# Hybrid decoder step on one core: the prompt mixer and the sample mixer in one block

## The chip, the cores and the metric

The kernel runs on one core of a Trainium2 chip, in one launch. A core has TensorE (PE; its weight loads are shown as PEld), VectorE (DVE), ScalarE (ACT), GpSimd (POOL) and SyncE (SP), each with its own instruction stream, and 16 DMA engines that serve all their transfers. The engines meet only through semaphores: an instruction waits until a semaphore has reached a value, and adds to one when it is done. The metric is device time in microseconds (us); lower is better. A time is the median of several runs.

## The reference

One layer of a decoder, applied to a prompt of 512 tokens and to a sample group of 8 x 4 = 32 tokens, which share all weights:

```python
def trunk_layer(x, c, ada_w, ..., state):
    mod = (jax.nn.silu(c) @ ada_w + ada_b)[:, None, :]
    sh1, sc1, gt1, sh2, sc2, gt2 = jnp.split(mod, 6, axis=-1)
    h = rmsnorm(x, g_mix) * (1 + sc1) + sh1
    mix, new_state = token_mixers(h, w_in, w_out, gate_b, mh_g, sinks, conv_w, state)
    x = x + gt1 * mix
    h = rmsnorm(x, g_ffn) * (1 + sc2) + sh2
    x = x + gt2 * peer_ffn(h, wq, subkeys, u_tab, v_tab)
    return x, new_state
```

`token_mixers` multiplies the normalised rows by `w_in` (1024 x 3336), runs three mixers on the result (an mLSTM with a matrix memory C, windowed attention with a key and value cache, a short convolution), and multiplies their outputs by `w_out`. For the prompt the states start at zero; for the sample they are inputs. `peer_ffn` chooses 128 of 16384 experts for each token (8 heads, 16 each, by the best sums of two lists of key scores), takes the dot product of the token with each chosen row of `peer_u`, and sums rows of `peer_v` with weights made of these dots. Everything is float32. The outputs are the rows of both groups and their new states.

## The kernel before

The kernel has three parts, one after the other, each a block with an instruction stream for each engine: `mix_prompt` (four tiles of 128 tokens), `mix_sample` (one tile of 32 rows), and `experts` (all tokens). A block ends when every engine has drained and all have met at a barrier (its rows carry the line of the `with` that opens the block, 934 and 1493); the next block begins there.

**A tile** is the same work in prompt and sample. Its rows are normalised (`dve_rms`), transposed in two batches T_H0 and T_H1 into hT (`transpose_rows`), and multiplied by seven column chunks of `w_in`, named GATES, QZ, KZ, VZ, SVCB, CCCH and OZ (`project`, line 618, and `transpose_weights`). The chunks alternate between the two banks ps_z[0] and ps_z[1], so a chunk waits until the one two before it has been copied out. GATES is copied out by VectorE in `dve_front` (line 785), CCCH there as well (line 826). The weights stream through three slots, in the order of `Stream`; a load waits until the matmuls on the chunk three before it are done. The last step is the out product (`out_product`, line 674) into both banks and the residual on VectorE (`dve_residual`, lines 874 to 878), which signals x1_ready; SP then stores the rows.

**Work for the experts done ahead.** While the mixers run, the kernel also does a part of the expert work of prompt tile 0: it routes the tokens (`keys`, `pairs`) and takes the 128 dots (`dots`, line 333). Each dot needs a gather of 128 rows of `peer_u`, 512 KB, issued by POOL (`gather`, line 341) into one of eight row buffers; a buffer is free when the dot on it is done. This work is put into named gaps of VectorE's stream. What a gap holds is set by the tables KEYS_IN, PAIRS_IN and DOTS_IN at line 274. Gap "Z" of the last prompt tile holds the keys and pairs of head 7 and 6 dots. Of the sample's gaps, "A" holds 7 dots, "B" 6, "C" 5, "D" 3, "E" 8, "F" 5, "G" 5, "K" 6, "L" 9, "N" 12, "O" 12, "Z" 11. VectorE runs them where the code has them, so what stands behind a gap waits for its gathers.

**The border.** VectorE's last work in the prompt block is gap "A", the residual of tile 3 and gap "Z" (lines 1294 to 1296). ScalarE and VectorE have by then normalised the sample's rows, and SP has loaded its first three weight chunks. SP's last work is to store the prompt's states and x1 and to wait for all of it (lines 1064 to 1067). The prompt's C is copied to the lower half of hT (`cT_out`) to be stored. The sample block begins with gap "A" on VectorE, the transposes on TensorE, the small loads, the rows and the weight chunks VZ, SVCB, CCCH and OZ on SP, and the gathers on POOL. Further on, SP loads the sample's key and value cache into `scratch`, which the routing work had used, and the sample's memory C (line 1515) into a weight slot, when the matmuls on OZ are done. TensorE transposes it at line 1695.

## Time and profile before

| | us |
|---|---|
| median of 3 runs | 2055.93 |
| lowest, highest run | 2049.76, 2057.97 |
| span of the profiled execution | 2046.0 |
| TensorE, weight loads busy | 1616.0, 764.0 |
| VectorE busy | 1207.7 |
| POOL busy | 1134.0 |
| ScalarE busy | 476.3 |

The page gives one execution from its first to its last instruction; it gives no other time of that execution than this span. Lines are those of the kernel before. In a row of a timeline the first number is the start in us from the span's start, the second how long it took; what stands in square brackets is how long the engine was idle just before it, and what ended that. The prompt mixer fills the span until 497, the sample mixer from 509 to 713, the experts the rest.

### The profile page before, as it was taken

To read this page: it belongs to the slowest core of one execution; us is meant where nothing else is said; L and a number is where in the kernel's file an instruction comes from. 1 tells how busy PE (TensorE), PEld (TensorE's weight loads), DVE (VectorE), ACT (ScalarE), POOL (GpSimd) and SP (SyncE) were. 2 spreads that over 40 slices of the span, in tenths; PEclk is the share of its full clock that TensorE was granted. 3 is DMA by queue.
4 is the path that set the end of the run, shared out by engine and by line. 5 is a ranking of instruction groups with operands and counts; after the bars stand their busy time and mean duration, and the time that the engine had idled before them with its cause. 6 is when DMAs were issued, how large, how long until landed. Compare 5 with 4: busy or idle time off the path is not lost.

```text
span 2046.0 us, 20838 instructions
## 1 busy us (share of the span) xinstructions
PE 1616.0 (79%) x5461; PEld 764.0 (37%) x5461; DVE 1207.7 (59%) x3129; ACT 476.3 (23%) x1217; POOL 1134.0 (55%) x1168
## 2 busy tenths in 40 slices
PE   6979989983767457768888888788878789599966
PEld 1524546451126113223433344333433344255422
DVE  2222355867766701116767766677667689679972
ACT  1221313130101021212223222222222223223321
POOL 3000021322873555777777667767777677577773
PEclk8989999996775679998999989899999899899988
DMA  8795676896995599999999999999999999799995
GB/s 319 254 364 207 215 263 218 305 337 135 355 385 179 198 401 404 392 416 394 400 420 420 400 368 418 419 373 420 420 401 391 388 403 419 308 412 417 414 372 226
DMA packets 237575, 713.43 MB, mean 349 GB/s; under 512 B 23102, under 2 KB 49056, under 8 KB 237457
## 3 DMA queue, kind: packets, MB, share of 16 engines
q0 software_dynamic: 156672, 570.49, 71.2%
q1 hardware_dynamic: 80488, 140.73, 19.4%
q10 hardware_dynamic: 312, 1.07, 0.2%
q8 instruction: 36, 0.59, 0.1%
q14 instruction: 67, 0.54, 0.1%
HBM read 704.42 MB, written 8.25 MB: 348 GB/s over the span
## 4 chain that ended last, share of the span: by engine, by line
PE 19%; DMA 14%; DVE 12%; issue 7%; POOL 7%; ACT 5%; DVEq 0%; POOLq 0%; ACTq 0%
PE ps_y L2316 13%; DVE u_rows L2095 6%; DMA v_rows<-in_peer_v_dram,expert_idx_ring 5%; DMA v_rows<-in_peer_v_dram,tile_idx 5%; PE ps_r L2290 4%; POOL u_rows L1890 3%; DMA u_rows<-in_peer_u_dram,expert_idx_ring 3%; POOL v_rows L1896 2%; POOL v_rows L1904 2%; ACT wt_diag L1987 2%; PE ps_y L2331 2%; DMA v_rows<-in_peer_v_dram,sample_idx 1%; DVE key_scores_w L2106 1%; ACT L2002 1%; ACT L2033 1%
## 5 line engine op out<-in xcount | busy, mean ns | idle before, releaser
L2316 PE MATMUL ps_y<-v_rows,wt_diag 128*128 128x512 f32 x1664 | 796.9, 621 | 146.6 <-DMA v_rows<-in_peer_v_dram,expert_idx_ring 65.2
L2316 PEld LDWEIGHTS ps_y<-v_rows,wt_diag 128*128 128x128 f32 x1664 | 311.4, 197 | 571.1 <-issue 547.5
L1890 POOL DMA_INDIRECT u_rows<-in_peer_u_dram,expert_idx_ring x384 | 368.2, 959 | 164.7 <-issue 90.3
L2095 DVE CUSTOM_DVE_ANT_0 u_rows<-u_rows,ps_y 128x1024 f32<-128x1024 f32 x360 | 420.4, 1218 | 64.1 <-DMA u_rows<-in_peer_u_dram,expert_idx_ring 58.1
L1896 POOL DMA_INDIRECT v_rows<-in_peer_v_dram,expert_idx_ring x384 | 366.7, 955 | 120.2 <-issue 99.3
L341 POOL DMA_INDIRECT low_rows<-in_peer_u_dram,tile_idx x128 | 174.7, 1364 | 214.7 <-DVE tile_dots L333 148.5
L607 PE MATMUL ps_z<-w_stream,hT 128*128 128x512 f32 (+5 forms) x560 | 249.0, 602 | 36.9 <-DMA w_stream<-in_w_in_dram 19.7
L2331 PE MATMUL ps_y<-v_rows,wt_diag 64*64 64x512 f32 x1024 | 135.1, 645 | 57.4 <-DMA v_rows<-in_peer_v_dram,tile_idx 50.8
L333 DVE CUSTOM_DVE_ANT_0 low_rows<-low_rows,tile_rows 128x1024 f32<-128x1024 f32 x128 | 152.9, 1232 | 44.1 <-DMA low_rows<-in_peer_u_dram,tile_idx 31.9
L607 PEld LDWEIGHTS ps_z<-w_stream,hT 128*128 128x128 f32 (+1 forms) x560 | 100.9, 185 | 163.9 <-issue 132.6
L1904 POOL DMA_INDIRECT v_rows<-in_peer_v_dram,tile_idx x128 | 122.1, 954 | 71.8 <-PE ps_y L2331 44.6
L2290 PE MATMUL ps_r<-wq,hT_next 128*128 128x256 f32 (+1 forms) x512 | 123.2, 396 | 17.9 <-ACT hT_next L1968 17.9
L1987 ACT ACTIVATE wt_diag<-ident,wts 128x128 f32<-128x128 f32 x416 | 127.2, 388 | 25.1 <-DVE wts L2101 25.1
L2105 DVE MAX8 top<-key_scores 128x8 f32<-128x128 f32 x64 | 18.2, 285 | 187.6 <-ACT key_scores L1978 187.4
L2290 PEld LDWEIGHTS ps_r<-wq,hT_next 128*128 128x128 f32 x512 | 101.9, 200 | 47.7 <-issue 22.6
L1983 ACT ACTIVATE act_val<-dots 128x8 f32<-128x8 f32 x52 | 10.9, 209 | 444.4 <-DVE dots L2095 444.3
L885 POOL TENSOR_TENSOR z_cc_ch<-z_cc_ch 128x256 f32<-128x256 f32 (+1 forms) x5 | 7.0, 1409 | 190.1 <-DVE z_cc_ch L826 190.0
L2331 PEld LDWEIGHTS ps_y<-v_rows,wt_diag 64*64 64x64 f32 x1024 | 39.6, 140 | 146.9 <-issue 114.8
L2095 DVE CUSTOM_DVE_ANT_0 u_rows<-u_rows,h_cur 128x1024 f32<-128x1024 f32 x24 | 28.7, 1227 | 89.0 <-DMA u_rows<-in_peer_u_dram,expert_idx_ring 88.9
L688 PE MATMUL ps_z<-w_out,qT_kT 128*128 128x512 f32 (+1 forms) x160 | 76.0, 636 | 4.7 <-DVE low_rows L1214 4.7
L894 POOL TENSOR_TENSOR z_o<-z_o,mlstm_g 128x512 f32<-128x512 f32 (+1 forms) x5 | 7.2, 1431 | 82.5 <-ACT z_o L755 82.5
L1996 ACT ACTIVATE wt_diag<-half_ident,tile_dots 128x64 f32<-128x64 f32 x128 | 32.2, 335 | 81.8 <-PE ps_y L2331 81.3
(434 smaller groups left out, 1628.3 us busy)
## 6 DMA issues: line engine op xcount, KB each, us to landing
w_stream<-in_w_in_dram SPq DMA_DIRECT2D x25, 2048.0 KB, 12.8
w_stream<-in_ada_w_dram SPq DMA_DIRECT2D x12, 2048.0 KB, 12.8
w_stream<-in_peer_wq_dram SPq DMA_DIRECT2D x8, 1024.0 KB, 8.5
wq<-in_peer_wq_dram SPq DMA_DIRECT2D x4, 2048.0 KB, 42.2
w_stream<-in_w_in_dram SPq DMA_DIRECT2D x5, 1568.0 KB, 8.5
w_stream<-in_w_in_dram SPq DMA_DIRECT2D x5, 1536.0 KB, 17.5
u_rows<-in_peer_u_dram,expert_idx_ring POOLq DMA_INDIRECT x384, 7.4
v_rows<-in_peer_v_dram,expert_idx_ring POOLq DMA_INDIRECT x384, 7.9
```

The costliest lines, as they stand in the source:

```text
L333: self.nc.vector.tensor_tensor_reduce(self.rows[:, k % NB, :], self.rows[:, k % NB, :], self.X.h0[:, :], 1.0, 0.0, ALU.mult, ALU.add, self ...
L341: self.nc.gpsimd.indirect_dma_start(self.rows[:, k % NB, :], None, U, bass.IndirectOffsetOnAxis(self.keep["idx0"][:, k:k + 1], 0)).then_in ...
L607: mm = self.nc.tensor.matmul(X.ps_z[i % 2][0:n, 0:b - a], X.hT[:, kc, 0:n], X.wr[:, slot, kc, 0:b - a], start=(kc == 0), stop=(kc == KC - 1))
L688: mm = nc.tensor.matmul(X.ps_z[c][0:n, :], X.mixT[:, kc, 0:n], X.w_out[:, kc, c * 512:(c + 1) * 512], start=(i == 0), stop=(i == KC - 1))
L1890: g.indirect_dma_start(u_rows[:, j, :], None, U, bass.IndirectOffsetOnAxis(where[:, j:j + 1], 0))\
L1896: g.indirect_dma_start(v_rows[:, j, :], None, V, bass.IndirectOffsetOnAxis(where[:, j:j + 1], 0))\
L1904: g.indirect_dma_start(v_rows[:, j, :], None, V, bass.IndirectOffsetOnAxis(idx0[:, k:k + 1], 0))\
L1987: a(diag[:, par, j, :], K["ident"][:, :], ACT.Copy, scale=wts[:, par, j:j + 1])\
L2095: v.tensor_tensor_reduce(u_rows[:, j, :], u_rows[:, j, :], row[:, :], 1.0, 0.0, ALU.mult, ALU.add, dots[:, par, j:j + 1]).then_inc(s["u_us ...
L2290: mm = nc.tensor.matmul(ps_r[:, 0, 0:256], hT[:, kc, :], wq[:, kc, bass.ds(h * 256, 256)], start=(kc == 0), stop=(kc == KC - 1))
L2316: mm = nc.tensor.matmul(ps_y[:, c * 512:(c + 1) * 512], diag[:, par, j, :], v_rows[:, j, c * 512:(c + 1) * 512], start=(first and j == 0), ...
L2331: mm = nc.tensor.matmul(ps_q[b * HP:(b + 1) * HP, half, c * 512:(c + 1) * 512], diag[rows, i % 2, j + b, 0:HP], v_rows[rows, j + b, c * 51 ...
```

## The change

The sample mixer is no longer a block of its own. `mix_sample` returns a function for each engine, and the prompt block calls it where that engine's prompt work ends. In place of the barrier there are waits for what both parts use: TensorE waits for tile 3's x1_ready and pool_done before the first chunk; SP waits for x1's store before it loads the sample's rows over the same buffer, for the small states before it stores C_p, and for the routing (a_routed) before it loads the caches; ScalarE and VectorE wait for the stores of the prompt's states before they copy SVCB and GATES. C_p is stored from `dm` (d_matrix) in place of hT. On VectorE the copy of the upper half of hT, and with it `dve_front`, now stands ahead of gap "Z" of tile 3 and of the sample's gap "A", which are called from inside it (`behind_rows`).

```diff
-        self.cT_out = self.hT[:, 0:4, :]
+        self.cT_out = self.dm[:, :, :]
...
+SMALL_STATES = 4 + MH
...
         self.z_landed(act, SVCB)
+        if self.kind == "sample":
+            act.wait_ge(self.prompt["state_out"], 16 * (1 + SMALL_STATES))
...
-    def dve_front(self, dve, chain, K):
+    def dve_front(self, dve, chain, K, behind_rows=None):
...
         v.tensor_copy(X.hT[:, 4:8, 0:n], X.ps_t[:, :, 0:n]).then_inc(s["t_free"], 1)
+        if behind_rows:
+            behind_rows(dve)
         self.gap(dve, "B")
         self.z_landed(dve, GATES)
+        if self.kind == "sample":
+            dve.wait_ge(self.prompt["state_out"], 16 * (1 + SMALL_STATES))
...
+            sp.wait_ge(done, 16 * SMALL_STATES)
             sp.wait_ge(s["t_free"], NT * TB + 1)
             sp.dma_start(O["C_p"].rearrange("l b h v k -> v (l b h) k"), X.cT_out).then_inc(done, 16)
             store(NT - 1)
             load_row(sp, nc, mod, X.row_g, 2, True, S.s["small_in"])
-            sp.wait_ge(done, 16 * (5 + MH))
-            sp.wait_ge(s["x1_stored"], 16 * (1 + NT))
+            sample["sync"](sp)
+            sp.wait_ge(done, 16 * (1 + SMALL_STATES))
...
             A.gathers(pool, U, NT - 1, "Z")
+            sample["gpsimd"](pool)
...
+            sample["scalar"](act)
...
                 T.dve_residual(dve, chain)
-                T.gap(dve, "Z")
+                if more:
+                    T.gap(dve, "Z")
...
+            def left_of_last_tile(eng):
+
+                T = tile(NT - 1)
+                T.chain0 = chain0
+                T.gap(eng, "Z")
+
+            sample["vector"](dve, left_of_last_tile)
...
+            pe.wait_ge(s["t_free"], NT * TB + 1)
+            sample["tensor"](pe)
...
-    with nc.Block() as block:
-        @block.sync
-        def _(sp):
+    def on_sync(sp):
...
+        sp.wait_ge(before["x1_stored"], 16 * (1 + NT))
+        sp.dma_start(X.xr[0:NS, :], I["x_sample"].rearrange("b t d -> (b t) d")).then_inc(s["xr_in"], 16)
+        for i in range(RING, len(CHUNKS)):
+            X.stream.load(sp, I, "sample", i)
+        sp.wait_ge(before["a_routed"], PH)
+        sp.dma_start(kc, I["cache_swa_k"][0].rearrange("b w h d -> w b (h d)")).then_inc(s["k_in"], 16)
...
+        def behind_rows(eng):
+
+            left(eng)
+            T.gap(eng, "A")
+
+        T.dve_front(dve, chain, K, behind_rows)
...
+        T.transpose_rows(pe, K)
+        pe.wait_ge(before["x1_ready"], NT)
+        pe.wait_ge(before["pool_done"], NT)
+        T.project(pe, K)
...
+    return {"sync": on_sync, "gpsimd": on_gpsimd, "scalar": on_scalar, "vector": on_vector, "tensor": on_tensor}
...
-            mix_prompt(nc, I, O, mod, x1_dram, X, K, s, S)
-            mix_sample(nc, I, O, mod, x1_dram, X, K, s2, S)
+            S.prompt = s
+            sample = mix_sample(nc, I, O, mod, x1_dram, X, K, s2, S, s)
+            mix_prompt(nc, I, O, mod, x1_dram, X, K, s, S, sample)
```

What the order of the instructions becomes is shown at three places. Lines of the changed kernel are shifted by a few (878 becomes 885, 1515 becomes 1536). First VectorE, from the residual of tile 3 on (z_q and z_k are scratch rows there, swa_scores holds the rows of x, and line 426 is the first of the routing work in gap "Z"); before:

```order
L874 TENSOR_TENSOR z_q<-ps_z,mod_gate 128x512
L875 TENSOR_TENSOR z_k<-ps_z,mod_gate 128x512
L877 TENSOR_TENSOR swa_scores<-swa_scores,z_q 128x512
L878 TENSOR_TENSOR swa_scores<-swa_scores,z_k 128x512
L426 MAX scratch<-scratch 128x8
```

And with the change:

```order
L881 TENSOR_TENSOR z_q<-ps_z,mod_gate 128x512
L882 TENSOR_TENSOR z_k<-ps_z,mod_gate 128x512
L884 TENSOR_TENSOR swa_scores<-swa_scores,z_q 128x512
L885 TENSOR_TENSOR swa_scores<-swa_scores,z_k 128x512
L784 COPY hT<-ps_t 128x4x32
L426 MAX scratch<-scratch 128x8
```

The copy of hT, which stood behind gap "Z", the border and gap "A" at line 781, has moved up to directly behind the residual. Next TensorE, from the prompt's last out product to the sample's third chunk, with the semaphores that are waited for (mix_ are the prompt's, smp_ the sample's); before:

```order
L688 MATMUL ps_z<-w_out,qT_kT 128x512 x8
L934 UNCONDITIONAL_BRANCH
L1663 UNCONDITIONAL_BRANCH [waits barrier_Pool_Activation_PE_DVE_SP_release]
L596 MATMUL ps_t<-ident,h 128x32 [waits smp_h_ready]
L596 MATMUL ps_t<-ident,h 128x32 x3
L596 MATMUL ps_t<-ident,h 128x32 [waits smp_t_free]
L596 MATMUL ps_t<-ident,h 128x32 x3
L607 MATMUL ps_z<-w_stream,hT 32x392 [waits mix_stream_in0,smp_t_free]
```

And with the change:

```order
L689 MATMUL ps_z<-w_out,qT_kT 128x512 x8
L597 MATMUL ps_t<-ident,h 128x32 [waits smp_h_ready,mix_t_free]
L597 MATMUL ps_t<-ident,h 128x32 x3
L597 MATMUL ps_t<-ident,h 128x32 [waits smp_t_free]
L597 MATMUL ps_t<-ident,h 128x32 x3
L608 MATMUL ps_z<-w_stream,hT 32x392 [waits smp_t_free,mix_stream_in0,mix_pool_done,mix_x1_ready]
```

The two branches with the barrier's wait are gone, and the first chunk has two waits more. Last SP, from the store of C_p to the first weight load of the sample block (x_rows is the store of x1, mod_gate the sample's gate row); before:

```order
L1061 DMA out_C_p_dram<-hT 128x4x128 [waits mix_t_free]
L962 DMA x_rows<-swa_scores 128x1024 [waits mix_x1_ready]
L900 DMA mod_gate<-mod_rows 32x1x1024
L934 UNCONDITIONAL_BRANCH [waits mix_row_out0,mix_row_out1,mix_x1_stored,mix_state_out]
L1494 UNCONDITIONAL_BRANCH [waits barrier_Pool_Activation_PE_DVE_SP_release]
L1498 DMA m_prev<-in_state_mlstm_m_dram 32x1x4
L1500 DMA sinks<-in_swa_sinks_dram 32x1 x4
L1502 DMA swa_scores<-in_x_sample_dram 32x1024
L257 DMA w_stream<-in_w_in_dram 128x8x512 [waits smp_zfull0]
```

And with the change:

```order
L1069 DMA out_C_p_dram<-d_matrix 128x4x128 [waits mix_t_free,mix_state_out]
L969 DMA x_rows<-swa_scores 128x1024 [waits mix_x1_ready]
L907 DMA mod_gate<-mod_rows 32x1x1024
L1517 DMA m_prev<-in_state_mlstm_m_dram 32x1x4
L1519 DMA sinks<-in_swa_sinks_dram 32x1 x4
L1522 DMA swa_scores<-in_x_sample_dram 32x1024 [waits mix_x1_stored]
L257 DMA w_stream<-in_w_in_dram 128x8x512 [waits smp_zfull0]
```

The waits that ended the block are gone from the middle; the wait for x1's store now stands at the load that overwrites its buffer, and the weight load is behind it.

## Rows read from the trace of the kernel before

**Rows 1.** The page's first row: the whole execution.
```profile
span 2046.0 us, 20838 instructions
```

**Rows 2.** Timeline of TensorE, 440 to 700: start, duration, line, tiles, count, [idle before].
```profile
468.24 7.03 PE L688 MATMUL ps_z<-w_out,qT_kT 128*128 128x512 f32 x16
509.12 0.61 PE L596 MATMUL ps_t<-ident,h 32*128 32x32 f32 x4 [33.84 <-PEq L934]
...
517.51 14.15 PE L607 MATMUL ps_z<-w_stream,hT 128*32 128x392 f32 x32 [6.79 <-DVE hT L781]
...
571.10 9.38 PE L607 MATMUL ps_z<-w_stream,hT 128*32 128x512 f32 x16 [4.97 <-DMA w_stream<-in_w_in_dram]
...
585.79 8.72 PE L607 MATMUL ps_z<-w_stream,hT 128*32 128x512 f32 x16 [4.05 <-DMA w_stream<-in_w_in_dram]
...
623.90 5.61 PE L1695 MATMUL ps_s<-ident,w_stream 128*128 128x128 f32 x28 [12.21 <-DMA w_stream<-in_state_mlstm_C_dram]
```

**Rows 3.** Timeline of VectorE, 480 to 585.
```profile
480.53 0.69 DVE L878 TENSOR_TENSOR swa_scores<-swa_scores,z_k 128x512 f32<-128x512 f32 x1
...
509.15 1.22 DVE L333 CUSTOM_DVE_ANT_0 low_rows<-low_rows,tile_rows 128x1024 f32<-128x1024 f32 x1 [11.98 <-PEq L934]
...
524.91 0.15 DVE L785 COPY z_gates_sq_sk<-ps_z 32x8 f32<-32x8 f32 x1
...
580.52 0.68 DVE L826 COPY z_cc_ch<-ps_z 32x512 f32<-32x512 f32 x1 [2.96 <-PE ps_z L607]
```

**Rows 4.** Instructions of line 934, the block's end: duration in ns, start.
```profile
L934 POOLq DRAIN  x1: 11095/11095/11095, 497.7 to 497.7; - x1
```

**Rows 5.** POOL's timeline, first gather behind "Z"; DMA issues 490 to 509: us to land.
```profile
492.21 1.18 POOL L341 DMA_INDIRECT low_rows<-in_peer_u_dram,tile_idx  x1 [21.07 <-DVE tile_dots L333]
...
low_rows<-in_peer_u_dram,tile_idx POOLq DMA_INDIRECT x6, 6.0
```

**Rows 6.** Busy time by stretch: engines, granted TensorE clock, DMA share, GB/s.
```profile
490.00:510.00 20.00, 0.61 (x4) 0.50 (x4) 7.99 (x15) 0.24 (x1) 7.96 (x6) 0.50 0.48 157
...
530.00:560.00 30.00, 21.20 (x56) 5.64 (x55) 18.95 (x38) 5.71 (x8) 25.42 (x16) 0.81 1.03 400
```

**Rows 7.** The dots alone (line 333) by stretch; each dot is two rows of x.
```profile
509.15:525.00 15.85, 15.31 (x26) 0.62 0.69 215
525.90:542.10 16.20, 9.84 (x16) 0.99 1.02 391
542.10:557.00 14.90, 9.81 (x16) 0.73 1.03 398
```

**Rows 8.** DMA, 525 to 553: packets, MB, share by queue; the gathers' us to land.
```profile
q0 software_dynamic: 1996, 7.28, 67.2%
q1 hardware_dynamic: 2037, 3.63, 34.8%
...
low_rows<-in_peer_u_dram,tile_idx POOLq DMA_INDIRECT x16, 9.0
```

**Rows 9.** SP's timeline, the store of x1; the same in the DMA view, 481 to 490.
```profile
481.24 0.33 SPq L962 DMA_DIRECT2D x_rows<-swa_scores  x1
...
x_rows<-swa_scores SPq DMA_DIRECT2D x1, 512.0 KB, 8.4
```

**Rows 10.** Timeline of SP, 524 to 600: the weight loads, the load of C.
```profile
524.83 14.52 SPq L257 DMA_DIRECT2D w_stream<-in_w_in_dram  x3
...
596.32 0.84 SPq L1515 DMA_DIRECT2D w_stream<-in_state_mlstm_C_dram  x1
```

**Rows 11.** DMA issues, 509 to 525: the load of VZ, KB, us to land.
```profile
w_stream<-in_w_in_dram SPq DMA_DIRECT2D x1, 2048.0 KB, 18.0
```

**Rows 12.** DMA, 596 to 624: C's load; 553 to 596: cache copies; 481 to 624: total.
```profile
w_stream<-in_state_mlstm_C_dram SPq DMA_DIRECT2D x1, 0.5 KB, 27.5
...
out_swa_k_s_dram<-in_cache_swa_k_dram SPq DMA_DIRECT2D x1, 496.0 KB
...
DMA packets 17156, 45.43 MB, mean 318 GB/s; under 512 B 1496, under 2 KB 4929, under 8 KB 17134
```

More of the change, by code:

```diff
@@ L1452, in sample_tile, with mix_sample @@
     return T
-def mix_sample(nc, I, O, mod, x1_dram, X, K, s, T):
+def mix_sample(nc, I, O, mod, x1_dram, X, K, s, T, before):
     W = X.scratch
@@ new lines, in on_sync @@
+    def on_sync(sp):
+        k_new, v_new = O["swa_k_s"][0], O["swa_v_s"][0]
+        sp.dma_start(X.mprev[0:NS, :], for_tokens(I["state_mlstm_m"][0])).then_inc(s["m_in"], 16)
+        for h in range(AH):
+            sp.dma_start(X.sink[h * NS:(h + 1) * NS, 0:1], I["swa_sinks"][0, h:h + 1].partition_broadcast(NS))\
+                .then_inc(s["sink_in"], 16)
+        sp.wait_ge(before["x1_stored"], 16 * (1 + NT))
[4 more added lines that the diff above has]
+        sp.dma_start(kc, I["cache_swa_k"][0].rearrange("b w h d -> w b (h d)")).then_inc(s["k_in"], 16)
+        sp.dma_start(vc, I["cache_swa_v"][0].rearrange("b w h d -> w b (h d)")).then_inc(s["kv_in"], 16)
+        sp.dma_start(nq, for_tokens(I["state_mlstm_n"][0].rearrange("b h k -> b (h k)"))).then_inc(s["small2_in"], 16)
+        sp.dma_start(n8, I["state_mlstm_n"][0].rearrange("b h k -> b (h k)")).then_inc(s["small2_in"], 16)
+        sp.dma_start(stc, I["state_conv"][0].rearrange("b w c -> (b w) c")).then_inc(s["small2_in"], 16)
+        sp.dma_start(k_new[:, 0:WIN - TS], I["cache_swa_k"][0, :, TS:WIN]).then_inc(s["y_stored"], 16)
+        sp.dma_start(v_new[:, 0:WIN - TS], I["cache_swa_v"][0, :, TS:WIN]).then_inc(s["y_stored"], 16)
+        stored = 2
+        T.z_landed(sp, CCCH)
+        T.z_landed(sp, OZ)
+        sp.dma_start(Cs, I["state_mlstm_C"][0].rearrange("b h v k -> v (b h) k")).then_inc(s["c_in"], 16)
+        T.z_out(sp, GATES)
+        T.z_out(sp, SVCB)
+        for b in range(B):
+            for new, rows in ((k_new, X.g5[b * TS:(b + 1) * TS, 264:392]), (v_new, X.g6[b * TS:(b + 1) * TS, 0:P])):
+                sp.dma_start(new[b, WIN - TS:WIN].rearrange("w h d -> w (h d)"), rows).then_inc(s["y_stored"], 16)
+                stored += 1
+        T.on(sp, "u_ready")
+        for j in range(CK - 1):
+            sp.dma_start(O["conv_s"][0, :, j], X.u[TS - CK + 1 + j:NS:TS, :]).then_inc(s["y_stored"], 16)
+            stored += 1
+        sp.wait_ge(s["n_ready"], 1)
+        sp.dma_start(O["n_s"][0].rearrange("b h k -> b (h k)"), n8).then_inc(s["y_stored"], 16)
+        sp.dma_start(O["m_s"][0], w8[:, 4:8]).then_inc(s["y_stored"], 16)
+        sp.wait_ge(s["cu_out"], 2 * MH)
+        sp.dma_start(O["C_s"][0].rearrange("b h v k -> v (b h) k"), Cs).then_inc(s["y_stored"], 16)
+        T.on(sp, "x1_ready")
+        sp.dma_start(x1_dram[SEQ:SEQ + NS, :], X.xr[0:NS, :]).then_inc(s["y_stored"], 16)
+        sp.wait_ge(s["y_stored"], 16 * (stored + 4))
@@ new lines, in on_gpsimd, with on_scalar @@
+    def on_gpsimd(pool):
+        A, U = X.ahead, I["peer_u"][0]
+        for w in "ABCDEFG":
+            A.gathers(pool, U, "sample", w)
+        T.pool_u(pool)
+        for w in "KLMN":
+            A.gathers(pool, U, "sample", w)
+        T.pool_og(pool)
+        A.gathers(pool, U, "sample", "O")
+        A.gathers(pool, U, "sample", "Z")
+    def on_scalar(act):
+        chain = Chain(act, s["act_step"])
+        chain.n = 1
+        a = nc.scalar.activation
+        T.act_front(act, chain)
+        for k, half in ((S_K0, 0), (S_K1, 4)):
+            T.t_landed(act, k)
+            a(kcT[:, half:half + 4, :], X.ps_t[:, :, :], ACT.Copy).then_inc(s["t_free"], 1)
+        act.wait_ge(s["sw_full"], 1)
+        for kv in range(KVH):
+            a(sT[:, kv * 2 * NS:(kv + 1) * 2 * NS], X.ps_n[kv][:, 0:2 * NS], ACT.Copy)
+            last = a(sN[:, kv * 2 * NS:(kv + 1) * 2 * NS], X.ps_n[kv][0:NS, P:P + 2 * NS], ACT.Copy)
+        last.then_inc(s["st_ready"], 1)
+        T.on(act, "sc_ready")
+        a(sc, sc, ACT.Exp, bias=X.smx[:, 1:2], accum_out=X.ssum[:, 0:1])
+        a(X.ses[:, 0:1], X.ses[:, 0:1], ACT.Exp).then_inc(s["swa_exp"], 1)
+        for i in range(0, B, 2):
+            act.wait_ge(s["ct_full"], i + 1)
+            a(CTs[:, 4 * i:4 * i + 4, :], X.ps_s[:, 0, :], ACT.Copy).then_inc(s["ct_even_out"], 1)
+        act.wait_ge(s["si_full"], 1)
+        a(intT, X.ps_n[1][:, 0:P], ACT.Copy).then_inc(s["int_ready"], 1)
+        T.act_norm(act, chain, X.ps_t[0:NS, :, :], lambda eng: T.t_landed(eng, S_I), "t_free")
+        T.on(act, "pv_full")
+        a(X.mixT[:, 4:6, 0:NS], X.ps_s[:, 0, 0:2 * NS].rearrange("p (a t) -> p a t", a=2), ACT.Copy)\
+            .then_inc(s["oa_ready"], 1)
```

392 lines of the change are left out of this document (156 added, 236 removed).

## The prediction

> **What bounds the kernel now.** I read the execution first as a whole and then at the one place where the change acts, the border between the prompt mixer and the sample mixer. The span is 2046.0 us [rows 1]; the sum below is made against it. The median of the runs shown is 2055.93 us, so 9.9 us lie outside the span, and I leave those as they are.
>
> At the border TensorE's row ends with the second half of the out product, 468.24 + 7.03 = 475.3 us, and the next matmul starts at 509.12 with 33.84 us idle before it [rows 2]. VectorE's row says that it went on until 497.2 (509.15 less 11.98 of idle time), doing gap "Z" of tile 3 behind the residual of 480.53 [rows 3]. So the stall has two sizes: 33.8 us on TensorE, 12.0 us on VectorE. What ended both is one row: POOL's DRAIN at the end of the block took 11095 ns from 497.7, that is until 508.8 [rows 4]. POOL drains because it had issued gathers from 492.21 on, which take 6.0 us to land [rows 5].
>
> The next question is whether the 33.8 us are on the path. They are not, as a whole. Behind the border the stage is held by the gathers and the DMA engines: from 530 to 560 they are full (share 1.03, 400 GB/s), while from 490 to 510 they were at 0.48 and 157 GB/s [rows 6]. VectorE's dots come in gathers' time: 8 dots (two rows each) in the 16.2 us from 525.9 and 8 in the 14.9 us from 542.1, so 2.03 and 1.86 us each, though a dot itself takes 1.22 us [rows 3, 7]. So what the change can give is earlier transfers, and the price is read from them.
>
> **The change part by part.** *The barrier goes* (the drains of all five engines, the release, the branches). TensorE can then transpose the sample's rows at 475.3, but its first chunk also needs tile 3's residual read out of the two banks (x1_ready, about 481.2) and the upper half of hT, which VectorE now copies directly behind the residual. The two chunks GATES and QZ took 14.15 us together [rows 2], so they would run from about 481.6 to 496 in place of 517.5 to 531.7: 35.9 us earlier. Nothing of that reaches the end yet, since the third chunk waits for the copy of GATES on VectorE, which stands behind the rest of gap "Z" and gaps "A" and "B".
>
> *Term 1, the copy of GATES.* Before, it is at 524.91 [rows 3]. Gaps A and B hold 13 dots. Eight rows are in flight at a time; six of them are used up by "Z", so two of the 13 are landed when Z ends, and the other eleven must come from gathers that POOL can only issue from 492.2 on. One end: they come as they did from 509.15 to 525.0, 13 dots in 15.85 us, 1.22 each [rows 7], and the whole idle time of 11.98 us goes. Other end: they share the DMA engines with the weights, which are now loaded at the same time: 492.2 + 10 x 1.86 + 9.0 to land [rows 8] + 1.2 for the dot = 521.0, a gain of 3.9. I take 3.9: the loads of VZ and SVCB, 2 MB and 1.5 MB, are issued at about 490.5 and 496 (SP has to wait for the store of x1, issued at 481.24 and 8.4 us to land [rows 9], and then for GATES and QZ); in a full stretch the hardware queue moved 3.63 MB in 28 us [rows 8], so they last until about 518.
>
> In that full stretch the two queues moved 1996 and 2037 packets, and the gathers' packets took 67.2% of the engines' time [rows 8]. The Trainium skill, "DMA: Bandwidth & Descriptors", section "Queues, rings and completion order", says that each DMA engine takes turns between the queues with work, a packet at a time; this speaks against the change, since every load that is moved up takes turns from the gathers that VectorE waits for. If turns were not taken and gathers went first, the sum would be 8 us better; the packet counts side with the rule.
>
> *Term 2, gaps C and D.* Before, their 8 dots took 16.2 us because VZ, SVCB and CCCH came in meanwhile (three issues from 524.83 on [rows 10]). Now VZ and SVCB are in, and CCCH can be issued only when the KZ chunk is through, some 8 us behind the copy of GATES. So about 6 of 8 dots run with no load beside them: 6 x (2.03 - 1.22) = 4.9. Ends: 0, and 8 x 0.81 = 6.5. I take 4.9.
>
> *Gaps E, F and G* I leave as they were. CCCH, OZ and the key and value caches follow each other on SP, so the hardware queue is never empty there; the ends are 0 and 4 us.
>
> *Term 3, two waits for weights.* VectorE waited 2.96 us for the CCCH chunk [rows 3], since TensorE had waited 4.97 us for its weights, and TensorE waited 4.05 us for OZ's [rows 2]. By my times CCCH would be issued at about 530 and wanted at 557 (behind gap E and the SVCB chunk), OZ issued at 541 and wanted at 570. A load that had only gathers beside it landed in 18.0 us [rows 11], so CCCH would be there at 548 and OZ, behind it, at 559 to 566. Both waits go: 3.0 + 4.05 = 7.0 us. If the cover is gone (loads as slow as before, 30 us) they stay: 0.
>
> *Term 4, the sample's memory C.* Its load is issued at 596.32 and TensorE had to wait 12.21 us for it until 623.9 [rows 2, 10]; it takes 27.5 us to land [rows 12]. It needs OZ's matmuls to be done and SP to be free, so it moves up by terms 1 to 3. Its own 27.5 us I take as unchanged. It could be 2.5 us less, as about 1 MB of cache copies queued right ahead of it (496 KB twice, at 400 GB/s [rows 6, 12]) would be through; it could also be 0.
>
> *Added waits.* SP waits for the small states before it stores C_p, and for x1's store before it loads the sample rows: queued behind it are the weight loads, which want GATES done (about 489) anyway, so the price is 1 to 2 us of a load that has slack. TensorE's waits for x1_ready and pool_done are due at 481 and earlier. VectorE and ScalarE wait for the stores of the states before they overwrite them: those are issued before 470 and wanted at about 520, so nothing. If one of these stores took 50 us, VectorE would stand with all gaps queued behind it; no row comes near. C_p is stored from d_matrix in place of hT, the same copy.
>
> *Behind C* I expect the same work in the same time as before: transposes, gaps N, O and Z, the drain, the experts. *Sum:* 3.9 + 4.9 + 7.0 + 0 = 15.8 us; 2055.9 - 15.8 = 2040.
>
> **A check by bytes.** From 481 to 624, when C is there, the DMA engines moved 45.43 MB at a mean of 318 GB/s [rows 12]. At the 400 GB/s of the full stretch they take 113.6 of those 143 us. So 29 us is what the change could give if the DMA engines never fell idle and C's load were as dense as the rest. The sum stays well below, as it should with a stretch (518 to 530) in which only gathers run and with C's load as slow as before.
>
> **The rivals.**
> *A. The gathers set the pace and give it back.* Term 1 holds, but C and D stay at 2.0 us a dot, and the OZ load is late again because SP stands in the cache loads. Gain 2 to 10, at 5: 2051. For it: dots at 1.86 us in a stretch in which only one load ran; TensorE's clock may also be halved in a wait from 496 to 521, as it was from 490 to 510 (0.50 [rows 6]), and a chunk like OZ then costs up to 7 us more on the path. Against it: both loads have some 27 us for what takes 18 us.
> *B. The transfers are lighter than I think.* The loads fit into the idle share of 490 to 510, term 1 gives its 12 us, G ends without a queue. Gain 24 to 31, at 27: 2029. Against it: the byte check, which it all but uses up.
> *C. Slower.* Loads beside gathers cost more than turns. Place: the gathers from 492 on. At 1.86 us apart it is my forecast; from 2.25 us on the copy of GATES is no earlier than before (492.2 + 22.5 + 10.2 = 524.9). If the spacing stays at 2.5 us through the 35 dots from C to L, these cost 35 x 0.5 = 17 us more, and the two waits return 7: about +10 to +15, 2068. Against it: the fullest stretches show 1.86 and 2.03.
> *D. The engines still meet.* One of the new waits works as the barrier did (VectorE's for the stored states, say). Then the border costs what it did: 2056.
>
> **How the numbers follow.** About 0.5% (10.3 us) is what a measurement of this kernel can tell from no change. Forecast (gain 10.3 to 24): 0.59, all faster. A: 0.22, nearly all within 0.5%. B: 0.11, faster. C: 0.05, slower. D: 0.03, same. So faster 0.70, same 0.25, slower 0.05. The range leaves out half of B's tail and the worse half of A with C and D: 2027 to 2052.
>
> **What would show it.** Right: no row idle for a block's end near 500; GATES' matmuls at about 482 and its copy on VectorE at 519 to 522; dots of C and D under 1.7 us apart; no DMA wait ahead of CCCH and OZ; the load of C issued near 580 and everything behind it 16 us earlier. Wrong: the copy of GATES at 513 (B) or behind 525 (C); a wait for weights ahead of OZ (A); VectorE or ScalarE idle until a state's store (D). My own weakest step is term 2, as it needs an empty hardware queue for some 10 us.

## The result, and the profile after

The changed kernel takes 2038.14 us (median of 7 runs) against 2055.59 us for the kernel before (7 runs beside them). The ratio is 0.9937, with a 95% interval of 0.9916 to 0.9957: 9 to 17 us faster. A second set, 9 runs against 30, gives 2043.11 against 2052.89 us and 0.9948 (0.9915 to 0.9982). The forecast of 2040 us was right in direction and size. Several of its terms were not, and they made up for each other.

Each run lasts 1.7 to 2.2 us longer than its span. The profiled execution of after has a span of 2036.3 us, the one of before 2046.0 [rows 1]; that one was quick for its kernel, for a second execution of before has 2053.1.

The rows of after follow. First TensorE's timeline (start, duration, line, tiles, count, [idle before]); it answers to [rows 2]:

```profile
482.96 15.00 PE L608 MATMUL ps_z<-w_stream,hT 128*32 128x392 f32 x32 [5.23 <-DVE hT L784]
519.23 0.53 PE L597 MATMUL ps_t<-ident,z_gates_sq_sk 32*128 32x32 f32 x3 [21.27 <-DVE z_gates_sq_sk L795]
...
560.46 7.05 PE L608 MATMUL ps_z<-w_stream,hT 128*32 128x512 f32 x16
571.45 9.88 PE L608 MATMUL ps_z<-w_stream,hT 128*32 128x512 f32 x16
610.30 6.76 PE L1719 MATMUL ps_s<-ident,w_stream 128*128 128x128 f32 x32 [7.51 <-DMA w_stream<-in_state_mlstm_C_dram]
```

GATES and QZ run at 482.96 in place of 517.51. TensorE then waits 21.27 us for the copy of GATES: most of the 33.84 us has only moved. The CCCH chunk (560.46) and OZ (571.45) no longer wait for weights. VectorE's timeline, which answers to [rows 3]:

```profile
481.81 0.69 DVE L885 TENSOR_TENSOR swa_scores<-swa_scores,z_k 128x512 f32<-128x512 f32 x1
482.42 0.28 DVE L784 COPY hT<-ps_t 128x128 f32<-128x128 f32 x1
...
518.50 0.15 DVE L792 COPY z_gates_sq_sk<-ps_z 32x8 f32<-32x8 f32 x1
...
529.57 1.23 DVE L333 CUSTOM_DVE_ANT_0 low_rows<-low_rows,tile_rows 128x1024 f32<-128x1024 f32 x1 [4.06 <-DMA low_rows<-in_peer_u_dram,tile_idx]
...
536.21 0.15 DVE L806 SCALAR_TENSOR_TENSOR gate_lf<-gate_pre,gate_log 32x4 f32<-32x4 f32 x1
...
570.20 0.67 DVE L833 COPY z_cc_ch<-ps_z 32x512 f32<-32x512 f32 x1
```

The residual's last row starts at 481.81, 1.28 us later than before, so from here on marks are counted from that row. The copy of GATES is at +36.7 (before +44.4), the copy of CCCH at +88.4 (+100.0). In gap D, whose first dot is the row at 529.57, VectorE waited 4.06 us for gathered rows. SP's timeline, and behind the dots the DMA view of 490 to 512 (us to land):

```profile
483.92 0.38 SPq L1069 DMA_DIRECT2D out_C_p_dram<-d_matrix  x1
...
581.49 0.84 SPq L1536 DMA_DIRECT2D w_stream<-in_state_mlstm_C_dram  x1
...
w_stream<-in_w_in_dram SPq DMA_DIRECT2D x1, 2048.0 KB, 8.2
w_stream<-in_w_in_dram SPq DMA_DIRECT2D x1, 1536.0 KB, 11.5
```

VZ and SVCB land in 8.2 and 11.5 us; C's load is issued at 581.49, 14.8 us earlier than before.

All executions side by side, in us behind tile 3's residual. "C and D" is the time from the copy of GATES to gate_lf, so the 8 dots of these gaps; "experts" is where SP issues the first load of the expert part, and the next column how long that part lasts. A ratio is taken against runs of the kernel before that were made beside that kernel, so the medians of different rows are compared by their ratios.

| kernel | GATES copied | C and D | load of C | transposes of C | experts | their part | median (runs) | ratio (95%) |
|---|---|---|---|---|---|---|---|---|
| before | 44.4 | 17.1 | 115.8 | 143.4 | 234.3 | 1331.2 | 2055.59 (7) | |
| before_again | 45.1 | 18.1 | 114.6 | 143.3 | 234.5 | 1336.0 | 2055.12 (1) | |
| after | 36.7 | 17.7 | 99.7 | 128.5 | 214.6 | 1339.9 | 2038.14 (7) | 0.9937 (0.9916 to 0.9957) |
| again | 37.9 | 14.5 | 96.3 | 126.8 | 216.4 | 1340.4 | 2043.11 (9) | 0.9948 (0.9915 to 0.9982) |
| late_copy | 36.1 | 16.1 | 107.6 | 134.1 | 220.4 | 1342.2 | 2049.53 (10) | 0.9981 (0.9963 to 0.9998) |
| pool_hold | 42.3 | 17.6 | 104.0 | 134.5 | 220.6 | 1337.5 | 2046.50 (10) | 0.9976 (0.9955 to 0.9996) |
| late_weights | 37.3 | 17.4 | 107.8 | 131.9 | 223.2 | 1343.1 | 2048.55 (10) | 0.9976 (0.9954 to 0.9998) |
| breath_front | 36.8 | 11.3 | 91.7 | 125.1 | 212.9 | 1336.2 | 2029.58 (4) | 0.9877 (0.9841 to 0.9913) |
| breath_all | 37.3 | 11.3 | 92.9 | 126.1 | 214.3 | 1329.0 | 2032.64 (4) | 0.9903 (0.9866 to 0.9940) |
| early_c | 36.5 | 16.2 | 79.6 | 119.4 | 209.4 | 1337.3 | 2031.63 (4) | 0.9881 (0.9840 to 0.9922) |
| early_breath | 36.7 | 11.3 | 80.1 | 111.7 | 199.0 | 1330.9 | 2018.65 (4) | 0.9811 (0.9756 to 0.9865) |
| all_three | 36.9 | 11.3 | 79.8 | 111.5 | 198.6 | 1335.1 | 2020.20 (4) | 0.9822 (0.9773 to 0.9871) |
| before_breath | 44.7 | 11.3 | 115.1 | 135.7 | 222.4 | 1331.3 | 2042.34 (10) | 0.9944 (0.9927 to 0.9962) |
| before_both | 44.3 | 11.3 | 101.8 | 131.3 | 217.7 | 1335.9 | 2039.81 (4) | 0.9931 (0.9909 to 0.9953) |

The two spans differ by 9.7 us: 19.7 gained from the residual to the experts, 1.3 lost ahead of it, 8.7 lost in the experts' part, in which no line was changed.

### The profile page after: what moved, and what is told of

Same layout as the page of the kernel before. It is cut to its first block, busy times and chain, and to the rows that moved or that the text cites. A ratio compares the mean times of both kernels' runs of the same rounds, so it can differ in the third digit from the quotient of the medians.

```text
span 2036.3 us, 20831 instructions
## 1 busy us (share of the span) xinstructions
PE 1605.8 (79%) x5461; PEld 757.2 (37%) x5461; DVE 1209.1 (59%) x3129; ACT 476.2 (23%) x1217; POOL 1115.8 (55%) x1168
## 4 chain that ended last, share of the span: by engine, by line
PE 19%; DMA 17%; DVE 10%; issue 8%; POOL 8%; ACT 4%; DVEq 0%; POOLq 0%; ACTq 0%
PE ps_y L2342 12%; DMA v_rows<-in_peer_v_dram,expert_idx_ring 6%; DMA v_rows<-in_peer_v_dram,tile_idx 6%; DVE u_rows L2121 5%; DMA u_rows<-in_peer_u_dram,expert_idx_ring 5%; POOL u_rows L1916 4%; PE ps_r L2316 3%; POOL v_rows L1922 3%; PE ps_y L2357 2%; POOL v_rows L1930 2%; ACT wt_diag L2013 1%; DVE key_scores_w L2132 1%; ACT L2028 1%; ACT L2059 1%; DVE top_i L2134 0%
## 5 line engine op out<-in xcount | busy, mean ns | idle before, releaser
L2342 PE MATMUL ps_y<-v_rows,wt_diag 128*128 128x512 f32 x1664 | 787.5, 614 | 164.9 <-DMA v_rows<-in_peer_v_dram,expert_idx_ring 77.6
L2342 PEld LDWEIGHTS ps_y<-v_rows,wt_diag 128*128 128x128 f32 x1664 | 306.2, 195 | 585.2 <-issue 561.8
L341 POOL DMA_INDIRECT low_rows<-in_peer_u_dram,tile_idx x128 | 163.3, 1276 | 213.7 <-DVE tile_dots L333 127.5
L333 DVE CUSTOM_DVE_ANT_0 low_rows<-low_rows,tile_rows 128x1024 f32<-128x1024 f32 x128 | 153.1, 1232 | 36.5 <-DMA low_rows<-in_peer_u_dram,tile_idx 35.8
## 6 DMA issues: line engine op xcount, KB each, us to landing
w_stream<-in_w_in_dram SPq DMA_DIRECT2D x5, 1536.0 KB, 11.5
```

The costliest lines, as they stand in the source:

```text
L333: self.nc.vector.tensor_tensor_reduce(self.rows[:, k % NB, :], self.rows[:, k % NB, :], self.X.h0[:, :], 1.0, 0.0, ALU.mult, ALU.add, self ...
L341: self.nc.gpsimd.indirect_dma_start(self.rows[:, k % NB, :], None, U, bass.IndirectOffsetOnAxis(self.keep["idx0"][:, k:k + 1], 0)).then_in ...
L2342: mm = nc.tensor.matmul(ps_y[:, c * 512:(c + 1) * 512], diag[:, par, j, :], v_rows[:, j, c * 512:(c + 1) * 512], start=(first and j == 0), ...
```

## Where the transfers went: three experiments on the border

The theory was that of the prediction: the change gives earlier transfers. Its rival: only POOL's drain mattered, and the early chunks and loads give nothing.

**again**, the changed kernel once more.

> The changed kernel, unchanged, a second execution. All marks are counted from the end of tile 3's residual on VectorE (481.81 in the first execution of after, 480.53 before). First execution of after: copy of GATES +36.7, dots of gaps C and D 16.7 us, load of C issued +99.7, experts begin +214.6, experts' part 1339.9 us (before: 1331.2). In the middle of C's dots one gather on POOL took 6.40 us. If that gather is a matter of chance, it is elsewhere now, C and D take 11 to 13 us and C's load is issued at +95 to +97, as term 2 of the prediction had it. If the program causes it, it is back at the same gather and all marks are within 2 us. If the longer experts' part comes from the change, it is again 8 to 9 us over 1331; if it is the spread between executions, it lies anywhere from 1328 to 1345.

A long gather (one that POOL takes unusually long to issue) is back in gap C, with 6.39 us, and the experts' part at 1340.4, so neither looks like chance. It is one gather later than in after, but beside the same dots. C and D took 14.5 us in place of 17.7, and C's load came 3.4 us earlier, so the marks were not within the 2 us expected: that is their spread.

**late_copy** keeps VectorE's old order, without the barrier:

```diff
-        T.dve_front(dve, chain, K, behind_rows)
+        behind_rows(dve)
+        T.dve_front(dve, chain, K)
```

> Only the barrier goes; VectorE has the order of before, with the copy of hT behind gaps Z and A, so TensorE's first chunk starts late and the loads of VZ and SVCB behind it. Theory (the gain is earlier transfers, the loads among them): the gathers have the DMA engines to themselves, so the copy of GATES comes at +33 (after: +36.7), but the loads are late again, the waits ahead of CCCH and OZ come back with about 7 us, and C's load is issued at +103 to +105 (after: +99.7; before: +115.8); about 0.996 of before. Rival (the gain is POOL's drain alone, and early chunks and loads only disturb the gathers): copy at +33 and everything behind it early by the same 3 to 4 us, C's load at +96; about 0.992.

**late_weights** keeps the early chunks and holds the loads back:

```diff
+        T.z_out(sp, GATES)
         for i in range(RING, len(CHUNKS)):
             X.stream.load(sp, I, "sample", i)
```

> The changed kernel, but SP loads VZ, SVCB and CCCH only when GATES has been copied out, as late as before; TensorE's first two chunks stay early. Theory: no load beside the gathers of gaps A and B, so the copy of GATES is at +32 to +34 (term 1's other end); then the loads run beside the gathers of C, D and E, the waits ahead of CCCH and OZ return with about 7 us, C's load is issued at +102 to +105. Rival (the early loads give nothing): copy at +33, C's load at +96.

TensorE's timeline of late_weights, the CCCH and the OZ chunk:

```profile
564.56 9.27 PE L608 MATMUL ps_z<-w_stream,hT 128*32 128x512 f32 x16 [5.18 <-DMA w_stream<-in_w_in_dram]
579.39 6.12 PE L608 MATMUL ps_z<-w_stream,hT 128*32 128x512 f32 x10 [4.30 <-DMA w_stream<-in_w_in_dram]
```

Both waits are back in both kernels (late_copy: 6.13 and 5.78 us), C's load comes 8 us later than in after, the experts 4 to 9 us later than in the two executions of the changed kernel. Of the 17.2 us that the change gives at C's load (means of the two executions of each kernel) 9.7 hang on the early loads, and the early chunks are worth what they do for these. The rival, with C's load at +96, is out. But two numbers are wrong in both expectations. C's load came about 3 us behind the end of the range (+105). And with no load beside them the gathers were to bring the copy of GATES to +32 to +34, and it stayed at +36 to +37. Without the loads, then, something else holds it back.

**pool_hold** gives POOL alone its pause back:

```diff
+        first = DOTS_AT[(NT - 1, "Z")] + NB
+        for k in range(first, first + DOTS_IN[(NT - 1, "Z")]):
+            pool.wait_ge(A.u_in[k % NB], 16 * (k // NB + 1))
         for w in "ABCDEFG":
```

> The changed kernel, but POOL waits until the six gathers of gap Z have landed before it issues those of gap A, as its drain made it do before; the other engines go on. Theory (the price of the pause is only what the DMA engines lose by it, and they have the weight loads to do): Z's rows land at about +26, eight gathers go out at once, and the copy of GATES is at +37 to +40; C's load at +100 to +103. Rival (the drain is the whole of what the barrier cost): the copy comes 11 to 12 us later, at +47, and C's load at +110.

POOL's timeline: the last gather of Z and the first of A.

```profile
501.61 0.94 POOL L341 DMA_INDIRECT low_rows<-in_peer_u_dram,tile_idx  x1 [0.30 <-issue]
510.87 1.10 POOL L341 DMA_INDIRECT low_rows<-in_peer_u_dram,tile_idx  x1 [8.32 <-DMA low_rows<-in_peer_u_dram,tile_idx]
```

A pause of 8.32 us costs 5.6 us at the copy of GATES and 4 to 8 at C's load, between theory and rival. So the pause that the drain had put into POOL's work is worth some 6 of the 17 us.

## The long gather

The stretch where term 2 should have come in, in POOL's timeline of after, and behind the dots the DMA engines' share (tenths) and GB/s in 40 slices of 517.69 to 528.09:

```profile
518.41 0.98 POOL L341 DMA_INDIRECT low_rows<-in_peer_u_dram,tile_idx  x1 [0.30 <-issue]
519.69 6.40 POOL L341 DMA_INDIRECT low_rows<-in_peer_u_dram,tile_idx  x1 [0.30 <-issue]
526.39 0.93 POOL L341 DMA_INDIRECT low_rows<-in_peer_u_dram,tile_idx  x1 [0.30 <-issue]
...
DMA  9999999999999999999310000000000000194879
GB/s 441 394 394 457 362 425 425 378 410 378 394 457 362 441 410 410 441 394 362 126 47 0 0 0 0 0 0 0 0 0 0 0 0 0 32 205 79 205 299 378
```

One gather took 6.40 us to issue where its neighbours took under 1, and for some 3 us of it no DMA engine moved a byte. Meanwhile VectorE ran its dots without a gap:

```profile
519.48 1.21 DVE L333 CUSTOM_DVE_ANT_0 low_rows<-low_rows,tile_rows 128x1024 f32<-128x1024 f32 x1
520.62 1.21 DVE L333 CUSTOM_DVE_ANT_0 low_rows<-low_rows,tile_rows 128x1024 f32<-128x1024 f32 x1
521.77 1.21 DVE L333 CUSTOM_DVE_ANT_0 low_rows<-low_rows,tile_rows 128x1024 f32<-128x1024 f32 x1
```

They start 1.14 us apart, the next one before the last has ended. In the eight executions without a pause there are ten gathers of over 4 us in the sample mixer: nine beside dots that run so, and one of 4.58 us (late_weights, 641.10) beside four multiplications in a row, which begin at 640.25 and end at 644.87. In gap Z of tile 3, where dots run so as well, gathers take up to 1.99 us. Where the dots are 1.28 us apart, each begun after the last has ended (512.23 to 518.50 in after), they take 0.96 to 0.98. So the theory became: a gather's issue is held up while VectorE works without a gap. The rival was a fetch of POOL's code, since one packet of an instruction queue lies in that stretch (not in the 6.40 us themselves, though one lies in the 6.39 us of again).

The edit makes VectorE wait behind each dot until it has ended, which is the pause of the kernels below (breath_front: in Z and A to D; breath_all: in all the sample's gaps):

```diff
             ....then_inc(self.s["a_used"], 1)
+            if (t, w) in [(3, "Z")] + [("sample", g) for g in "ABCD"]:
+                dve.wait_ge(self.s["a_used"], k + 1)
```

> The changed kernel; in gap Z of tile 3 and the sample's gaps A to D VectorE waits after each dot until that dot is done, about 0.1 us without an instruction in it. Theory (POOL's issue of a gather is held up while VectorE runs dots back to back: 1.99 us in gap Z, 6.40 us in gap C, 0.94 us where VectorE pauses between dots): the gathers of gap A are issued 1.25 to 1.3 us apart in place of 2.29, none takes over 2.5 us; the copy of GATES comes at +33 to +36 (after: +36.7 and +37.9), C and D take 11 to 13 us (17.7 and 14.5), C's load is issued at +91 to +95 (99.7 and 96.3); about 0.991 of before. Rival (the long gather is a fetch of POOL's code, of which the DMA view shows one packet there, or a full ring): it stays at the same gather with 6.4 us, all marks 1 us later by the pauses; 0.995.

> As breath_front, with the pause after each of the dots of all the sample's gaps. Theory: the marks up to C's load as there; where the gathers set the pace (E to L) the pause costs nothing, since VectorE waits for rows; in N, O and Z it costs up to 0.1 us for each of 35 dots and saves the stalls of 4 to 5 us that four of seven executions show in gap Z: experts at +205 to +211 (after: +214.6 and +216.4); 0.988 to 0.992 of before. Rival: the pauses only add up, experts at +217 to +220, 0.996.

POOL's timeline of breath_front:

```profile
495.42 0.97 POOL L343 DMA_INDIRECT low_rows<-in_peer_u_dram,tile_idx  x1 [0.30 <-issue]
...
523.32 0.96 POOL L343 DMA_INDIRECT low_rows<-in_peer_u_dram,tile_idx  x1 [0.30 <-issue]
524.58 1.19 POOL L343 DMA_INDIRECT low_rows<-in_peer_u_dram,tile_idx  x1 [0.30 <-issue]
...
528.62 4.46 POOL L343 DMA_INDIRECT low_rows<-in_peer_u_dram,tile_idx  x1 [0.30 <-issue]
```

The same dots on the same rows: no long gather in the gaps with the pause, and one of 4.46 us in gap E, which has none. C and D take 11.3 us. In the five kernels with the pause in all gaps no gather takes more than 2.09 us. The rival is out: the pause leaves POOL's instructions as they were.

The traces show more of the link. Of the 958 gathers that POOL begins while a dot runs (sample mixer, all fourteen traces), 949 end 0.8 to 0.9 us after the end of a dot. As a rule it is the dot that was running; a gather of over 4 us lets three or four such ends pass first. The Trainium skill, "SBUF — State Buffer", section "SBUF: two separate sides", says that VectorE and GpSimd share a pair of ports under a lock held for a whole instruction, so that during a VectorE instruction in a two-port mode GpSimd cannot write the descriptors of its DMAs, and the DMA engines idle; of an instruction with two inputs in SBUF, as a dot has, it says that it contends only with a GpSimd instruction that reads SBUF. The trace agrees in what it shows, the 6.40 us and the idle engines. That it is this port no run here shows, and why one gather gets through at the end of the first dot (1.99 us) and another lets four ends pass, is open.

The pause did not move the copy of GATES (+36.8, expected +33 to +36). The busy times of four stretches say why (share and GB/s of the DMA engines are the last two columns). The first two are of breath_front, then come 25 us of after and the same 25 us, from +12 to +37, of late_weights:

```profile
490.00:520.00 30.00, 7.41 (x18) 1.86 (x17) 26.36 (x48) 3.56 (x5) 22.93 (x20) 0.62 1.03 397
520.00:530.00 10.00, 8.56 (x21) 2.13 (x20) 9.79 (x20) 0.59 (x1) 7.87 (x8) 0.94 1.02 409
...
493.81:518.81 25.00, 4.15 (x10) 0.88 (x8) 20.75 (x39) 1.87 (x2) 20.43 (x16) 0.67 1.04 402
...
492.45:517.45 25.00, 4.20 (x10) 0.88 (x8) 20.11 (x35) 1.87 (x2) 20.73 (x15) 0.67 0.79 256
```

Gathers and loads together fill the DMA engines, with the pause (breath_front) and without it (after). In late_weights, without the loads, they are not full, and the copy comes no earlier: there POOL's issue sets the pace, one gather behind the other. So two limits lie at the same place, the DMA engines with the loads and POOL's issue without them. Taking away one of them, as late_weights and breath_front do, gives nothing there; no run takes away both in the changed kernel.

Of breath_front's 5 to 8 us in front of C little reached the end: C's load now lands in 33 us, TensorE waits 13.11 us for it, and the experts begin 2 to 4 us earlier than in after. breath_all missed its +205 to +211 in the same way (+214.3).

## The wait for C, and what the change is worth without it

**early_c** loads C into SVCB's slot, ahead of the value cache:

```diff
-    Cs = X.wr[:, 0, :, :]...
-    CTs = X.wr[:, 1, :, :]...
+    Cs = X.wr[:, 1, :, :]...
+    CTs = X.wr[:, 0, :, :]...
...
+        T.z_landed(sp, SVCB)
+        sp.dma_start(Cs, I["state_mlstm_C"][0]...).then_inc(s["c_in"], 16)
         sp.dma_start(vc, ...)
         sp.dma_start(k_new[:, 0:WIN - TS], ...)
         sp.dma_start(v_new[:, 0:WIN - TS], ...)
-        T.z_landed(sp, CCCH)
-        T.z_landed(sp, OZ)
-        sp.dma_start(Cs, I["state_mlstm_C"][0]...).then_inc(s["c_in"], 16)
```

> The changed kernel with the sample's memory C loaded into the weight slot of SVCB in place of OZ's (its transposes go to OZ's slot), as soon as SVCB's matmuls are done, and ahead of the value cache and the two cache copies. Theory (behind the border the DMA engines set the pace up to C's transposes, and TensorE's wait for C, 6 to 7.5 us in both executions of after, is the last of it): C's load is issued at +78 to +82 (after: +99.7), lands 26 to 30 us later at +106 to +110, TensorE no longer waits for it, but for the dots of gap L: transposes of C at +117 to +120 (after: +128.5), experts at +204 to +208; 0.990 of before. Rival (the DMA engines are full from +10 to +125, so a load that goes earlier pushes the gathers back by as much): L's dots end 5 us or more later than the +120 of after, the transposes come at +126 or later, 0.994 to 0.996.

The transposes come at +119.4 with no wait for C, the experts at +209.4, 5 to 7 us earlier than in after and again (1.4 us behind the range). The rival wanted the transposes at +126 or later: C's load was late, not only one of many.

> early_c and breath_all together. If the two act on different waits (the pause keeps the gathers going up to gap G, 6 to 8 us; the early load takes away TensorE's wait for C, 13 to 16 us in the kernels with the pause), C's load is issued at +70 to +74 behind tile 3's residual, the transposes of C come at +110 to +114 (after +128.5, early_c +119.4, breath_all +126.1), experts at +199 to +203; 0.983 to 0.986 of before. If both only move the same bytes and the DMA engines set the pace from +10 on, the transposes stay at +118 or later and experts at +207 or later; 0.988.

TensorE's timeline of early_breath:

```profile
596.96 4.26 PE L1720 MATMUL ps_s<-ident,w_stream 128*128 128x128 f32 x20 [1.50 <-DMA w_stream<-in_state_mlstm_C_dram]
```

The two edits add up: transposes at +111.7, experts at +199.0, 2018.65 us. This is the fastest kernel of the study, 0.9811 of before. C's load was not earlier than in early_c (+80.1, expected +70 to +74), as SP stood 15.71 us in the issue ahead of it, that of the states n.

**all_three** adds two small things: the cache copies moved behind the small stores, and SP's wait for the small states, which SP had stood in until 483.92, taken away.

> early_breath, and the two copies of the sample's caches to the outputs (0.5 MB each) are issued behind C and all small stores, and SP no longer waits for the small states before it stores C_p. By the bytes (1 MB at 400 GB/s less ahead of gap L's dots) the transposes of C come 2.5 us earlier than in early_breath, experts 2 to 3 us earlier. If the copies went through in idle time anyway, no difference. SP's wait, 16 us long, should be worth nothing: C_p's store moves from +2 to -12, the load of VZ stays at +9.

Neither gives anything (+111.5 and +198.6): C_p's store moved to -12.1, the load of VZ stayed at +8.6, and the cache copies had cost nothing.

**before_breath** and **before_both** put the pause, and the pause with the early load, into the kernel before.

> The kernel before, with the pause after each dot of gap Z and of the sample's gaps, the barrier kept. It tells what the pause is worth without the change. If the pause only helps where no load runs beside the gathers and the rows are there ahead of VectorE, it has nothing to act on behind the border (copy of GATES at +44 to +46 behind tile 3's residual, C and D 17 us, the waits ahead of CCCH and OZ stay at 1 to 5 us, C's load at +114 to +117) and saves only the stall of 5 to 6 us in the last gap: experts at +228 to +232 (before: +234.4), 0.997 of before; the change is then worth 14 to 17 us on top of it (breath_all: +214.3). If the pause helps the gathers everywhere, C's load comes at +108 or earlier.

> The kernel before with the pause and the early load of C, the barrier kept; against early_breath (experts at +199.0) it tells what the changed border alone is worth once the gathers and C are out of the way. If the DMA engines, full from the border on, set the pace, the border's 12 us of idle VectorE and idle DMA come through whole with the two waits for weights behind them: transposes of C at +128 to +132, experts at +215 to +220, so 16 to 21 us for the change. If the early load of C takes up the slack, the difference is under 10 us: experts at +209 or earlier.

The stretch of gaps A and B in before_breath; without the pause it had a share of 0.69 and 215 GB/s [rows 7]:

```profile
514.40:530.20 15.80, 8.21 (x17) 2.40 (x18) 14.63 (x25) 0.00 (x0) 12.05 (x12) 0.57 0.85 309
```

I had expected nothing there. The gathers now come in time, 12 in place of 9, so the rows of C and D have landed when VectorE gets there, and C and D take 11.3 us although the weights load beside them. The weights pay: the waits ahead of CCCH and OZ grow to 7.46 and 5.21 us, and C's load is where it was (+115.1). It then lands in 20.6 us, and the experts begin 12 us earlier. The pause alone is worth as much as the change (0.9944 and 0.9937).

Between kernels that have the pause in both, the change moves the experts by 8 us (222.4 to 214.3); with the early load as well, by 19 us (217.7 to 199.0; 2039.81 and 2018.65 us), inside the 16 to 21 expected. Without the slack that C's late load leaves, the border comes through whole.

## The 4.8 us given back among the experts

In the executions of after the experts' part is 1339.9 and 1340.4 us, in those of before 1331.2 and 1336.0.

> The kernel before, a second profiled execution, for the length of the experts' part: 1331.2 us in the first one, 1337.5 to 1343.1 in the five executions with the changed border. If the change lengthens the experts' part, it is again 1329 to 1333. If the first one was only a quick execution, it is 1336 to 1344. The mixers' part should be the same as in the first: copy of GATES at +44 behind tile 3's residual, C's load at +114 to +117, experts at +233 to +236.

The second execution, at 1336.0, lies at the edge of the second answer, so I compared the parts gather by gather. From the 435th gather to the 440th the changed kernel loses 5 us, at one instruction of VectorE. Its timeline in before, after and breath_all:

```profile
1311.19 1.28 DVE L2208 SCALAR_TENSOR_TENSOR x<-x,final_stat,final_g 128x1024 f32<-128x1024 f32 x1
1316.94 0.17 DVE L2101 TENSOR_TENSOR wts<-act_val,expert_gate 128x8 f32<-128x8 f32 x1 [4.46 <-issue]
```

```profile
1296.43 1.28 DVE L2234 SCALAR_TENSOR_TENSOR x<-x,final_stat,final_g 128x1024 f32<-128x1024 f32 x1
1306.99 0.17 DVE L2127 TENSOR_TENSOR wts<-act_val,expert_gate 128x8 f32<-128x8 f32 x1 [9.27 <-issue]
```

```profile
1293.32 1.28 DVE L2236 SCALAR_TENSOR_TENSOR x<-x,final_stat,final_g 128x1024 f32<-128x1024 f32 x1
1299.07 0.17 DVE L2129 TENSOR_TENSOR wts<-act_val,expert_gate 128x8 f32<-128x8 f32 x1 [4.46 <-issue]
```

VectorE waits for nothing that the profile shows ("issue"), 9.25 to 9.29 us in all six executions of the changed border without the pause and 4.44 to 4.65 in the other eight. It is the only such wait over 3 us of VectorE among the experts. What the six have in common is VectorE's code up to there; that it waits for its own code, while the DMA engines are full (416 GB/s), I hold likely and have not shown. It returns 4.8 us of the gain, and the kernels with the pause, whose wait is the short one, have these 4.8 us in their medians beside what the pause does in the mixer. The rest of the difference between the parts is within the spread: 1329.0 to 1336.2 in the executions with the short wait.

## Why the prediction came out right

Gains are means of the two executions of each kernel, counted from the residual.

*The outside of the span.* I put 9.9 us outside it. It is about 2; the rest was that the profiled execution was quick. The sum, made of differences, is not touched.

*Term 1*, the copy of GATES: 3.9 predicted, 7.5 measured. The first of the eleven gathers went out 11.9 us behind the residual (forecast 11.7), the eleventh at +30.2 in the first execution (forecast 30.3) and +28.0 in the second. What was mis-sized is above all the 9.0 us that the last one takes to land: it took 5.3 and 8.7 us. The step behind it that failed is that VZ and SVCB would last to 518, which is 37 us behind the residual: the later of them landed at +27.7 and +32.4. VZ landed in 7.6 to 8.8 us in all eight executions that load it early, with the pause or without; there it goes out 2 to 3 us ahead of the first gather. SVCB took 11.5 to 16.9 us in those without the pause and 17.7 to 17.9 in those with it. That the gathers would be issued 1.86 us apart came out in the first execution (1.83), but not for the reason given: POOL's issue was held up in gap Z (1.99 us each). With the pause they are issued 1.3 us apart.

*Term 2*, gaps C and D: 4.9 predicted, 1.5 measured (none in the first execution). The hardware queue was empty, as forecast, and a gather stood still. The reason was wrong too: what set the pace of the 8 dots was not the loads beside them, but whether POOL had issued their gathers in time (before_breath: 11.3 us with the loads beside them). With the pause the term is there in full, 6.3 us.

*Gaps E to G* unchanged, *term 3* 7.0: from gate_lf to C's load 8.2 measured. Both waits went, for the reason given; late_weights and late_copy bring them back.

*Term 4*, C's load unchanged: it landed 1.4 us slower, and TensorE still waited 7.5 and 6.3 us for it.

*Added waits*: nothing, as forecast; all_three shows it for the longest, SP's.

*Behind C* the same time: wrong in both directions. 3.1 us were gained up to the experts, in one execution 4.8 and in one 1.4, where a long gather in the last gap came or did not; 4.8 us were lost to VectorE's wait for issue.

So 18.9 us up to the experts (7.5 + 1.5 + 8.2 - 1.4 + 3.1) and 4.8 returned leave 14, against 15.8 forecast and 9 to 17 measured. That the two lie so close is luck: term 1 and the stretch behind C gave 6.7 us more than forecast, term 2 gave 3.4 less, and VectorE's wait among the experts, which was not in the sum, took 4.8. What held is the mechanism of earlier loads, term 3. Rival A describes what happened to C and D and was wrong on OZ. B's condition came about in the first execution (both loads were in by 510), but the copy of GATES did not gain B's 12 us. C and D did not come about; C's price counts 35 dots from C to L where the gaps hold 41, which changes nothing else.

## What to carry to other kernels

When engines are let run on past a border, ask which queue gets the time first: here half of the gain came from weight loads that could start early, and TensorE's 33.8 us of idle time were mostly idle again behind it. An engine that issues DMAs in software can be held up by another one that never pauses: look for long issue rows beside back-to-back work, and try a wait for the end of each such instruction before moving any transfer. A transfer that is late although it has an earlier free buffer is worth moving, but only together with what feeds the engines beside it: up to the experts the pause alone gave 0 to 4 us in the changed kernel, the early load 5 to 7, both 16 to 17.
